# A hybrid decoder trunk on one core: weight tiles loaded in pairs of 1 MB

## The reference, cut to what matters

```python
def reference(x, ...):
    for layer in range(DEPTH):                       # DEPTH = 2
        if layer % 2 == 0:
            x = attention_layer(x, ...)              # q/k/v projection, two kinds of attention, w_out
        else:
            x = sgu_layer(x, ...)                    # gelu(x w_in), gate by w_spatial, w_out
        x = peer_layer(x, ...)                       # 16384 single-neuron experts, top 16 for each of 8 heads

def peer_layer(...):                                 # per token block
    q = (xb @ w_query).reshape(-1, PEER_HEADS, 2, PEER_DKEY // 2)
    ...                                              # two top-16 over 128 keys each, top-16 of their sums
    idx = e1 * PEER_NKEYS + e2
    g = jax.nn.softmax(top, axis=-1)
    hid = jax.nn.gelu(jnp.einsum('td,thkd->thk', xb, expert_down[idx]))
    return jnp.einsum('thk,thkd->td', g * hid, expert_up[idx])
```

## Time and profile before

| what | value |
|---|---|
| median of 3 runs | 3370.4 us (3370.16 to 3371.86) |
| the profiled execution's own time | 3367.13 us |
| its span, first to last instruction | 3365.4 us |
| mean granted TensorE clock | 0.983 of full speed |
| PE busy (matmuls) | 3253.8 us, 97% |
| PE weight loads busy | 2985.9 us, 89% |
| POOL, DVE, ACT busy | 1883.4, 1842.0, 1412.1 us |
| DMA | 801.96 MB, mean 238 GB/s |
| chain that ended last | PE 78%, DVE 15%, issue 2%, DMA 1%, ACT 1%, POOL 1% |

### The profile page before, as it was taken

One profiled execution on the slowest core, in us unless ns is written; L12 is line 12 of the kernel. 1 busy time (PEld: TensorE's weight loads), 2 busy tenths in 40 slices (PEclk: granted clock), 3 DMA queues, 4 the chain that ended last, 5 costly groups with the idle time before them and its releaser, 6 DMA issues.

```text
span 3365.4 us, 48035 instructions
## 1 busy us (share of the span) xinstructions
PE 3253.8 (97%) x18712; PEld 2985.9 (89%) x18712; DVE 1842.0 (55%) x3786; ACT 1412.1 (42%) x2539; POOL 1883.4 (56%) x1079
## 2 busy tenths in 40 slices
PE   7878999998999999999999999999899999999999
PEld 6656799998999988888988878999899999888889
DVE  5365248997774544444422320889977744444443
ACT  3454223336886333333333232333388843333332
POOL 4312447886666455555354653588766664555552
PEclk9988999999999999999999999999999999999999
DMA  3200236787999788888632222478799997888883
GB/s 120 78 26 32 75 99 231 278 276 262 358 361 367 269 316 323 331 327 335 230 110 94 85 94 82 143 268 292 246 330 354 357 347 267 329 319 322 334 341 122
DMA packets 260226, 801.96 MB, mean 238 GB/s; under 512 B 23968, under 2 KB 73120, under 8 KB 259488
## 3 DMA queue, kind: packets, MB, share of 16 engines
q1 hardware_dynamic: 186272, 530.41, 44.9%
q0 software_dynamic: 73728, 268.47, 21.2%
HBM read 699.17 MB, written 99.61 MB: 237 GB/s over the span
## 4 chain that ended last, share of the span: by engine, by line
PE 78%; DVE 15%; issue 2%; DMA 1%; ACT 1%; POOL 1%; DVEq 0%; POOLq 0%; SPq 0%; ACTq 0%
PE banks L249 20%; PE banks L251 20%; PE banks L250 20%; PE banks L1154 5%; PE banks L1190 4%; DVE operand_lo L1302 1%; PE banks L264 1%; PE banks L266 1%; PE banks L265 1%; DVE operand_lo L1300 1%; DVE arena L1234 1%; DMA arena<-gate_scratch 1%; DVE gathered_rows L1234 1%; PE banks L1122 1%; DVE side L717 1%
## 5 line engine op out<-in xcount | busy, mean ns | idle before, releaser
L216 POOL TENSOR_TENSOR weights_lo<-raw_ring,weights_hi 128x1024 fp32r<-128x1024 f32 x498 | 1245.4, 2502 | 1117.3 <-ACT weights_hi L210 1116.0
L249 PE MATMUL banks<-operand_hi,weights_hi 128*128 128x384 f32 (+1 forms) x4648 | 1607.6, 346 | 12.2 <-POOL weights_lo L216 8.3
L250 PE MATMUL banks<-operand_lo,weights_hi 128*128 128x384 f32 (+1 forms) x4648 | 1586.6, 341 | 0.0
L251 PE MATMUL banks<-operand_hi,weights_lo 128*128 128x384 f32 (+1 forms) x4648 | 1586.4, 341 | 0.0
L249 PEld LDWEIGHTS banks<-operand_hi,weights_hi 128*128 128x128 f32 x4648 | 874.7, 188 | 90.7 <-issue 62.3
L210 ACT CAST weights_hi<-raw_ring 128x1024 fp32r<-128x1024 f32 x624 | 653.2, 1047 | 632.6 <-PE banks L251 559.6
L250 PEld LDWEIGHTS banks<-operand_lo,weights_hi 128*128 128x128 f32 x4648 | 874.9, 188 | 21.4 <-issue 1.4
L251 PEld LDWEIGHTS banks<-operand_hi,weights_lo 128*128 128x128 f32 x4648 | 874.2, 188 | 21.7
L1383 DVE TENSOR_TENSOR residual<-residual,banks 128x384 f32<-128x384 f32 x256 | 141.8, 554 | 662.0 <-PE banks L251 662.0
L1030 ACT ACTIVATE arena<-banks 128x384 f32<-128x384 f32 x256 | 125.9, 492 | 555.8 <-PE banks L251 548.7
L995 ACT CAST operand_hi<-arena 128x384 fp32r<-128x384 f32 x256 | 130.8, 514 | 278.8 <-DVE arena L1353 278.8
(11 more groups left out here) (191 smaller groups left out, 3055.8 us busy)
## 6 DMA issues: line engine op xcount, KB each, us to landing
raw_ring<-weight_tiles SPq DMA_DIRECT2D x624, 512.0 KB, 4.2
gate_scratch<-arena SPq DMA_DIRECT2D x24, 2048.0 KB, 13.4
arena<-gate_scratch SPq DMA_DIRECT2D x128, 384.0 KB, 7.5
hid_scratch<-arena SPq DMA_DIRECT2D x60, 768.0 KB, 7.4
arena<-hid_scratch SPq DMA_DIRECT2D x120, 384.0 KB, 5.7
arena<-up,side POOLq DMA_INDIRECT x146, 7.1
residual<-x_t SPq DMA_DIRECT2D x2, 1024.0 KB, 6.7
arena<-key_t SPq DMA_DIRECT2D x2, 1024.0 KB, 5.0
```

The lines of the kernel that those rows point to most:

```text
L216: eng.tensor_tensor(wl[:, b, :], raw[:, n % RING, :], wh[:, b, :].bitcast(F32), ALU.subtract).then_inc(done, 1)
L249: pe.matmul(out, w_hi, x_hi[:, c, :], start=start and c == 0, stop=False)
L250: pe.matmul(out, w_hi, x_lo[:, c, :], start=False, stop=False)
L251: last = pe.matmul(out, w_lo, x_hi[:, c, :], start=False, stop=stop and c == DC - 1)
```

## The change

Two neighbouring tiles are loaded by one DMA of 1 MB into slots 0 and 1 or 2 and 3 of the ring. The even tile's call issues it and waits for the lo parts of both tiles whose slots are overwritten; the odd tile's call does nothing. There are two semaphores, one for each half of the ring, and `split_hi` waits on that of its half. In the kernel there are then 312 weight DMAs of 1 MB instead of 624 of 512 KB.

```diff
-        raw_loaded = [sem(f"raw_loaded{b}") for b in range(RING)]
+        raw_loaded = [sem(f"raw_loaded{b}") for b in range(RING // 2)]
...
         def load_tile(sp, n):
 
+            if n % 2:
+                return
             if n >= RING:
                 wait_lo(sp, n - RING)
-            sp.dma_start(raw[:, n % RING, :], weight_tiles[n]).then_inc(raw_loaded[n % RING], 16)
+                wait_lo(sp, n + 1 - RING)
+            b = n % RING
+            sp.dma_start(raw[:, b:b + 2, :], weight_tiles[n:n + 2].rearrange("n p w -> p n w")).then_inc(raw_loaded[b // 2], 16)
 
         def split_hi(act, n):
 
             if n >= WRING:
                 act.wait_ge(tiles_done, n - WRING + 1)
-            act.wait_ge(raw_loaded[n % RING], n // RING * 16 + 16)
+            act.wait_ge(raw_loaded[n % RING // 2], n // RING * 16 + 16)
             act.copy(wh[:, n % WRING, :], raw[:, n % RING, :]).then_inc(hi_split, 1)
```

## The result

| | us |
|---|---|
| before, median of 4 runs on the same chip | 3370.39 (3370.16 to 3371.86) |
| after, median of 4 runs | 3390.04 (3389.33 to 3391.21) |
| ratio after / before, 95% | 1.0058 [1.0040, 1.0075] |
| after, the profiled execution: own time, span | 3389.33, 3387.6 |

The change costs 19.6 us, nearly three times the 6.7 us that a measurement can tell. The forecast was 3371.6, 1.2 us more than before, and the range ended at 3382: right in sign, far too small in size.

The account below looks back on a forecast made before the run. The prediction took TensorE to bound the kernel, with a matmul in flight 97% of the span. All terms were 0 but the first gather's 0.6 us, twice, so +1.2 us on the 3370.4 median gave 3371.6; range 3364 to 3382.

Parts of the forecast that it names:

- First gather: Start of the gathers, before DVE's routing: slower beside 1024 KB of weights, 0 to 2.0 us, taken as 0.6, twice 1.2.
- Stores of gates: Down phase, even places: go some 6 us later, one landing at 861.4 with its buffer wanted at 864.67; hidden.
- Stores of hidden slices: Routing stretch: up to 2.0 us later against 1.1 of cover, ACT's gelu up to 0.9 late; worth 0.
- The even tile's later issue: End of down: pair of tiles 174 and 175 lands 8.7 us after its issue, just before ACT's cast; worth 0.
- The last gate part: End of each down phase: keeps its place in the full queue; worth 0, ends 0 and 2.0 us.
- Up phase: Parts at even places go one lo part later, landing at 1224.2 against DVE's 1227.43; hidden by 3.2 us.
- Fewer issues: On SP: 312 DMA issues of 0.33 us leave an engine that mostly waits; worth 0.
- The signs: B: pairs over 13 us, ACT waiting, PE's waits for lo parts over 20; C: last gate part at 1096 or before.
- B: The ring runs dry in the full stretch at the end of down: 16 us, 3386; repeated 38 us, 3408; chance 0.07.
- C: The full stretch at the end of down drains sooner with larger DMAs: 13 us faster, 3357; chance 0.05.
- A: Weight bytes ahead of the first gather and the last gate part, both at upper ends: 8 us, 3378.4; chance 0.09.
- D: Everywhere: transfers are hidden and nothing moves; the forecast but for the gather's 1.2 us; chance 0.79 with the forecast.

Follow-up runs that it names:

- Experiment 5: Before, with an extra DVE reduction behind the wait for the first gather: of 1.76 us, 3381.64 against 3370.11; of 0.69 us, 3370.25 against 3370.00.
- experiment 4: After, with single tiles at down tiles 20 to 23: 3378.38 against 3369.68; before, with pairs at those tiles alone: 3383.80 against 3370.11.
- Experiments 2, 3 and 7: 2: before, pairs at down 70 to 127, 3377.80; 3: after, even-tile stores at old moment, 3384.03; 7: before, gate stores one tile later, 3376.88 (even), 3374.81 (all but last).
- experiment 2: Before, with pairs only outside the down phases: 3371.60; only at down tiles 0 to 69: 3382.04; only at 70 to 127: 3377.80; all against 3369.76.
- experiment 8: After, with single tiles at down tiles 20 to 23 and SP's other even-tile work between the pair's two waits: 3371.48 against 3370.11, ratio 1.0005.

## Why the prediction was wrong

*First gather: the step that failed first.* "So what the first gather loses, PE loses", at 0.6 us. Both halves were wrong. The gather lost 1.9 us, nearly the upper end of 2.0, as if all of the 512 KB more stood ahead of it; I took a number near the lower end because it had the engines to itself for its last 1.4 us. And the 1.9 us did not pass through one for one: 5.6 us per layer arrive, since DVE falls to the wrong side of POOL's subtractions, a price that is the same for a delay of another length and was met twice with no late gather. Experiment 5 shows it with no transfer touched, experiment 4 that it makes 11.7 to 13.7 us of the whole. With the right size and my rule the sum would have been 3370.4 + 2 x 1.9 = 3374.2, still "same". The rows of before had the warning: the earlier trace rows gives the routing as the one thing PE waits 9.3 us for, and DVE's 128x2048 operations take anything from 2.29 to 6.58 us. I costed a delay on DVE as its length, though the trace showed that the length of its instructions depends on when they start. Timeline of DVE in the kernel before, layer 0, a later block:

```profile
748.69 2.29 DVE L1300 TENSOR_TENSOR operand_lo<-side,constants 128x2048 fp32r<-128x2048 f32 x1
...
752.17 6.58 DVE L1302 TENSOR_TENSOR operand_lo<-operand_lo,side 128x2048 fp32r<-128x2048 f32 x1
```

The second found POOL in two subtractions, one behind the other (751.83 to 756.58), and ended 2.17 us after them.

The Trainium skill, "DMA: Bandwidth & Descriptors", section on queues, rings and completion order, has the engines take turns between the queues packet by packet, by which the gather would have lost nothing: 9.12 against 7.24 us does not agree with it here.

*Stores of gates: "Hidden", the second step that failed.* The landing was put at 846 + 13.4 + 2.0: a store 6.1 us late that takes 15.4 us, with 3.3 us of cover left. The same store, at 854.90 in the kernel after, was 7.9 us late and took 17.8. So the delay was short by 1.8 us and the landing by 2.4, together 4.2: 0.9 us more than the cover, and 0.9 us is what ACT waited. Neither alone would have used the cover up. The other five stores at the same place took 17.4 to 19.7 us; the 5.6 us late ones never held ACT up. Experiments 2, 3 and 7 give the gate loss 4.8 to 8.0 us. Why a later store also takes longer is argued only: other bytes stand in front of it in each case. It stays open.

*Stores of hidden slices.* ACT late "up to 0.9 us, once or twice per layer": it waited 27.1 us in 11, up to 3.5, so the size was far off; worth next to 0 was right all the same, as experiment 4 shows.

*The even tile's later issue* stood in what it is worth. The pair of tiles 174 and 175 landed in 9.6 us (8.7 predicted). The two pairs before it, DMA issues of the kernel after around 1077.4 and 1085.8 us:

```profile
raw_ring<-weight_tiles SPq DMA_DIRECT2D x1, 1024.0 KB, 9.4
...
raw_ring<-weight_tiles SPq DMA_DIRECT2D x1, 1024.0 KB, 10.1
```

ACT's casts waited 0.5 to 1.7 us for them, where the prediction had them land just before the cast. PE hardly waited: the 13.4 us to the point where PE would starve were not reached there. *The last gate part* kept its 14.4 to 14.8 us, as said. *Up phase* and *start*: hidden, +1.8 us within [-2.0, +4.4] in experiment 2. *Fewer issues*: 0, as experiment 8 shows.

*The signs.* The cast waited over 1 us for weights outside the end of down, five times in the routing stretches, up to 1.8 us; PE's wait for lo parts went to 17.7 us instead of staying near 8, and its wait for the routing was 8.5 and 10.1 us instead of 9.3 to 10. So three of the signs of being right failed, and none of those named for B or C came. The last gate part landed at 1110.8 instead of 1099 to 1102 because the whole stretch began later; its own time did not grow.

*The rivals.* B did not happen: the ring never ran dry. (Its long form adds up to (8.0 + 10.6) x 2 = 37 us, not 38.) C did not: the engines' rate in the full stretch stayed (412 GB/s against 413), and 1 MB per transfer bought nothing. A named the right place, and gave 3378.4: its second half did not come, and its first was worth 11 instead of 4 us. D was the forecast, and experiment 8 is what it takes to make it true in the median.

*The chances.* 0.83 on "same" rested on costs that were each compared with their cover one at a time and by medians. The earlier trace rows show the cover of one store; the others at even tiles were not looked at, and the landing time in a queue was raised by 2.0 us for the larger load in front, where the median rose by 5.6. A change that delays half the issues of a queue with such neighbours deserved 0.3 or more on slower.

## What to carry to other kernels

In an in-order issue queue a load that waits for two buffers holds back everything behind it: list what stands behind the wait, and compare its landing, sized in the new neighbourhood, with the buffer's next use, for every one of its kind. If a delay reaches an engine that shares something with another, cost it for both orders of arrival, since the price can be a step several times the delay. Such a step can also come by itself: look at the single executions of a repaired kernel, not at their median alone. And a wait list says who stood still, not what it cost: time between the same tiles of two traces found in one table what the list hid.

## What the hardware did that I had not expected

- DVE's 128x2048 operation with two SBUF inputs takes 2.29 us alone and 4.52 us if POOL's subtraction of 128x1024 started 0.03 us before it (4.24 if 0.34 us before); POOL's takes 4.19 instead of 2.40 us if DVE was 0.37 us ahead. A delay of 1.76 us per layer cost 5.8, one of 0.69 nothing that can be measured, and one execution paid 5.6 us in a layer with no such delay.
- A gather of 512 KB issued beside 1 MB and 768 KB took 9.1 us, beside 512 KB and 768 KB 7.2 to 7.3, and 5.6 and 4.9 with that store moved behind it.
- A store of 2 MB took 13.4 us in the median before and 19.0 after, in kernels that move the same bytes.
